# Feed-forward input products of a two-layer hybrid block: the high part of one weight unit is made ahead of the rounding of the inner values

## What is computed

```
def swiglu(h, w_in, w_out):
    g, u = jnp.split(h @ w_in, 2, axis=-1)
    return (jax.nn.silu(g) * u) @ w_out

fl = swiglu(rms_norm(xl, g_ffn_pre[i]) * (1.0 + sc2) + sh2, w_ffn_in[i], w_ffn_out[i])
xl = xl + gt2 * rms_norm(fl, g_ffn_post[i])
if need_ctx:            # the first layer only
    fc = swiglu(rms_norm(xc, g_ffn_pre[i]) * (1.0 + csc2) + csh2, w_ffn_in[i], w_ffn_out[i])
    xc = xc + cgt2 * rms_norm(fc, g_ffn_post[i])
```

## Time and profile before

| | |
|---|---|
| median of 3 runs | 1747.09 us (1743.40, 1747.09, 1752.45) |
| the profiled execution | 1751.41 us, its span 1749.6 us |
| mean granted TensorE clock | 0.991 |
| TensorE (PE) busy | 1677.9 us, 96% of the span |
| VectorE (DVE) | 709.6 us, 41% |
| ScalarE (ACT) | 641.9 us, 37% |
| GpSimd (POOL) | 678.1 us, 39% |
| chain that ended last | PE 82%, DVE 5%, issue 4%, ACT 4%, POOL 4%, DMA 1% |

### The profile page before, as it was taken

How to read it: one execution, slowest core, us unless ns; L and a number is a source line. 1 busy time by engine, 2 the same in 40 slices (tenths; PEclk the granted TensorE clock), 3 DMA queues, 4 the chain that set the end, 5 groups by cost and what they waited for, 6 DMA issues and landing times.

```text
span 1749.6 us, 25876 instructions
## 1 busy us (share of the span) xinstructions
PE 1677.9 (96%) x10242; PEld 1397.5 (80%) x10242; DVE 709.6 (41%) x1124; ACT 641.9 (37%) x1118; POOL 678.1 (39%) x454
## 2 busy tenths in 40 slices
PE   6999999999999999999899999999999999999997
PEld 4868887777877887878899878877887888888886
DVE  5135547707589635403455420015771451011103
ACT  4242126726422122213555342236762522222221
POOL 3211222038455545433542043335433444444443
PEclk9999999999999999999999999999999999999999
DMA  9553101023465645524556636432002353333331
GB/s 356 182 169 85 38 25 49 1 81 115 146 188 192 229 145 182 167 87 118 154 160 183 193 107 116 91 98 95 2 2 61 100 165 97 105 90 97 98 98 67
DMA packets 211987, 207.17 MB, mean 118 GB/s; under 512 B 16262, under 2 KB 180636, under 8 KB 211612
## 3 DMA queue, kind: packets, MB, share of 16 engines
q1 hardware_dynamic: 199208, 165.53, 31.6%
q10 hardware_dynamic: 12660, 39.99, 7.4%
HBM read 203.37 MB, written 2.13 MB: 117 GB/s over the span
## 4 chain that ended last, share of the span: by engine, by line
PE 82%; DVE 5%; issue 4%; ACT 4%; POOL 4%; DMA 1%; SPq 0%; ACTq 0%; POOLq 0%; DVEq 0%
PE ps L1722 38%; PE ps L1749 26%; PE ps L1900 3%; POOL w_lo L526 3%; PE ps L1956 3%; PE ps L2016 3%; PE ps L1921 3%; ACT w_hi L841 2%; PE ps L1796 1%; PE ps L1835 1%; DVE xs L1291 1%; DMA w_raw<-in_w_ffn_in 1%; PE ps L1968 1%; DVE hid_f L1310 1%; DMA mod_early<-in_w_mod 1%
## 5 line engine op out<-in xcount | busy, mean ns | idle before, releaser
L526 POOL TENSOR_TENSOR w_lo<-w_raw,w_hi 128x1024 fp32r<-128x1024 f32 (+1 forms) x221 | 558.5, 2529 | 892.4 <-ACT w_hi L841 892.2
L1722 PE MATMUL ps<-h_hi,w_hi 128*128 128x512 f32 (+1 forms) x1488 | 496.9, 352 | 11.9 <-POOL w_lo L526 8.1
L1722 PE MATMUL ps<-h_hi,w_lo 128*128 128x512 f32 (+1 forms) x1488 | 492.4, 349 | 0.0
L1722 PE MATMUL ps<-h_lo,w_hi 128*128 128x512 f32 (+1 forms) x1488 | 491.2, 349 | 0.0
L841 ACT ACTIVATE w_hi<-w_raw 128x1024 fp32r<-128x1024 f32 (+1 forms) x273 | 286.6, 1051 | 346.0 <-PE ps L1749 312.0
L1722 PEld LDWEIGHTS ps<-h_hi,w_hi 128*128 128x128 f32 x1488 | 269.9, 189 | 56.9 <-issue 20.8
L1722 PEld LDWEIGHTS ps<-h_hi,w_lo 128*128 128x128 f32 x1488 | 269.5, 189 | 36.1
L1722 PEld LDWEIGHTS ps<-h_lo,w_hi 128*128 128x128 f32 x1488 | 269.5, 189 | 35.7
L526 DVE TENSOR_TENSOR w_lo<-w_raw,w_hi 128x1024 fp32r<-128x1024 f32 x52 | 69.3, 1335 | 201.7 <-ACT w_hi L841 198.8
L1749 PE MATMUL ps<-w_hi,hid_hi 128*128 128x512 f32 x440 | 137.0, 393 | 8.0 <-ACT mod_row L853 4.2
L1310 DVE TENSOR_TENSOR hid_f<-silu_g,ps 128x512 f32<-128x512 f32 (+1 forms) x66 | 39.3, 595 | 254.2 <-PE ps L1722 253.8
(11 more groups left out here) (223 smaller groups left out, 1898.8 us busy)
## 6 DMA issues: line engine op xcount, KB each, us to landing
w_raw<-in_w_ffn_in SPq DMA_DIRECT2D x132, 512.0 KB, 3.8
w_raw<-in_w_ffn_out SPq DMA_DIRECT2D x66, 512.0 KB, 3.5
mod_raw<-in_w_mod ACTq DMA_DIRECT2D x42, 512.0 KB, 4.5
w_raw<-in_na_w_in SPq DMA_DIRECT2D x32, 512.0 KB, 3.7
mod_early<-in_w_mod SPq DMA_DIRECT2D x30, 512.0 KB, 9.8
full<-in_w_mod ACTq DMA_DIRECT2D x15, 512.0 KB, 5.1
w_raw<-in_ab_w_in SPq DMA_DIRECT2D x18, 256.0 KB, 5.9
w_raw<-in_ab_w_in SPq DMA_DIRECT2D x9, 512.0 KB, 8.9
```

Of the source, the lines that this page charges most:

```text
L526: eng.tensor_tensor(w_lo[:, u % RING, 0:width], w_raw[:, u % RAW, 0:width], w_hi[:, u % RING, 0:width].bitcast(F32), ALU.subtract).then_in ...
L1722: mm = pe.matmul(o[0], sta(x, o), mov(y, o), start=first and n == 0, stop=last and n == 2)
```

## The change

In ScalarE's `ffn_in` the call that makes the high part of unit s+2j+4 moves from behind the rounding `hid_hi` to in front of the wait for `hid_f`. The instructions stay the same in kind and number. The call carries its own waits: for the landing of its unit, and until TensorE has used unit s+2j+1, the up unit of the step. No transfer is issued by the moved lines. The change holds for all five input stages, 66 steps.

```
@@ -907,11 +907,10 @@
                         act.wait_ge(ff_full, f - 1)
                     act.activation(silu_g[:, f % 2, 0:width], ps(2 * (f % 2), 0, width), ACT.Silu)\
                         .then_inc(ff_silu, 1)
-                    feed(s + 2 * j + RING)
+                    feed(s + 2 * j + RING + 1)
                     act.wait_ge(ff_full, f + 1)
                     act.activation(hid_hi[:, j * width:(j + 1) * width], hid_f[:, f % 2, 0:width], ACT.Copy)\
                         .then_inc(ff_hi, 1)
-                    feed(s + 2 * j + RING + 1)
                     if hooks and j in hooks:
                         hooks[j]()
                     for m in late_loads.get((name, j), ()):
```

## The result

| | before | after |
|---|---|---|
| median of 7 runs beside each other | 1750.91 us (1743.40 to 1752.45) | 1755.59 us (1753.59 to 1758.15) |
| ratio, 95% interval | | 1.0043 (1.0026 to 1.0060) |
| profiled execution: time, span | 1751.41, 1749.6 us | 1754.93, 1753.1 us |
| mean granted clock | 0.991 | 0.989 |

The change costs 0.4% by the ratio. The two medians differ by less, 4.7 us or 0.27%, since the seven runs of before fall into two groups (1743.4 to 1747.1 and 1750.9 to 1752.5) and four of them lie in the upper one; the means differ by 7.1 us, 0.41%. In the later comparisons before's median was 1746.2 to 1747.1. The forecast was 1755.0 us, 0.45% over the median of three that it started from. Behind L908 the lines of after are one lower (L1721 is before's L1722, L1312 is L1313, L1748 is L1749).

A forecast was written before the change was run, and what follows sets the result against it. TensorE, busy 96% of the span, was taken as the bound, so changes matter only where it waits. Terms 3.4+2.5+2.2+1.1-3.9+2.6 = +7.9 us on the 1747.1 median gave 1755.0; its own range was 1750 to 1762.

The forecast's parts named there:

- Cycles of steps 0 to 7: fi0C: GpSimd's low part takes the port ahead of VectorE's urgent one, lengthening the two-step cycles; +3.4 us.
- First cycle: Steps 0 to 7 of fi0C: the odd unit TensorE waits for starts 1.9 us later, including +0.36 for hid_lo.
- Later cycles: Steps 0 to 7 of fi0C: each takes 14.9 us instead of 14.12, +0.8 in each of three.
- The doubtful step: Cycle's end in fi0C: who gets the port; requests 1.2 us apart in the steady cycle, 0.4 in the first.
- first rival: Copy is freed, port does not matter: fi0C cycle of transfer plus chain, 12.2 us; total -10.7, 1736.4 us; chance 0.13.
- Step 9: fi0C: TensorE's transposes wait longer for the modulation column that VectorE adds behind the held hid_lo; +2.5 us.
- Steps 10, 13, 16, 19: fi0C: late modulation delays silu, high part and VectorE's low part, 0.56 us short each time; +2.2 us for four.
- End of the stage: Last step of fi0C: VectorE, late from step 19, has h_lo and two low parts before the last hid_f; +1.1 us.
- Gains: fi0L: shorter mod_row waits (-0.7 twice), clock kept behind one (-1.6), shorter waits for sums (-0.9); together -3.9 us.
- Clock in `fi0C`: Longer TensorE waits in fi0C bring stretches of lower granted clock; between 0 and 5.2 us, middle taken, +2.6.
- Nothing moves: Rival: new blocks fall in slack, or fi0C losses equal the gains; 1747 us within 3; chance 0.20.
- Worse: Rival: every landing takes 5.1 us and clock is lost at all five waits; +14 to +16, 1762 us; chance 0.05.

The follow-up runs named there:

- e5_steps_0to7: New order only in steps 0 to 7 of fi0C, old order elsewhere, against the kernel before; 1747.86 us, run once.
- e1_long_only: New order only in the 512-token stages (fi0L, fi1L), old order in fi0C, against the kernel before; 1747.08 us, ratio 1.0003.
- e2_short_only: New order only in fi0C (256 tokens), old order in the other stages, against the kernel before; 1758.04 us, ratio 1.0061.
- e8_dve_first: New order in long stages and fi0C steps 0 to 7; in steps 1, 3, 5, 7 GpSimd's low part waits for VectorE's; 1737.68 us, ratio 0.9950 to before.
- e3_step9: New order only in step 9 of fi0C, old order elsewhere, against the kernel before; 1752.58 us, run once.
- e4_steps_10up: New order only in steps 10 to 21 of fi0C, old order elsewhere, against the kernel before; 1749.24 us, run once.

## Why the prediction was right

**The mechanism was the one forecast.** `hid_lo` of 128x256 is held, GpSimd's low part goes ahead of VectorE's in the first three cycles, all five waits of GpSimd's kind in `fi0C` vanish, and the column wait is 4.0. The first cycle in after, VectorE and then GpSimd:

```profile
814.22 2.44 DVE L1312 TENSOR_TENSOR hid_lo<-hid_f,hid_hi 128x256 fp32r<-128x256 f32 x1 [1.04 <-ACT hid_hi L912]
...
819.84 3.40 DVE L526 TENSOR_TENSOR w_lo<-w_raw,w_hi 128x1024 fp32r<-128x1024 f32 x1
```
```profile
819.72 2.44 POOL L526 TENSOR_TENSOR w_lo<-w_raw,w_hi 128x1024 fp32r<-128x1024 f32 x1 [2.38 <-ACT w_hi L841]
```

**Cycles of steps 0 to 7, forecast +3.4 without the clock.** e5_steps_0to7 has +3.45 from start to turn, with the turn's wait 0.15 shorter. But its waits up to the turn grew only by 1.5 us (9.3, against 7.8 in before and in e1_long_only), so some 2 us of this are slow stretches (820 to 828 at 0.80 and 0.77, 864 to 872 at 0.85 and 0.72): without them the term was too large. In after these waits even fell, from 7.8 to 6.7, and +0.7 in place with the clock in it is all that came.

First cycle: forecast +1.9, measured +1.5 (the start behind the wait lies 16.58 behind the stage's start, 15.04 in before). The term that failed is the 0.36 for `hid_lo` between the low part and the root. In after `post_norm` starts 1.01 behind the low part's end (817.38 behind 816.37), in before 0.94: `hid_lo` and the root run side by side, and it costs 0.07. Later cycles: forecast 14.9 each. The second of after takes 14.35 (838.64 to 852.99). The 0.36 is missing there too, and the moved high part starts 3.80 behind S and not 3.95, released by its landing, as forecast:

```profile
842.44 1.06 ACT L841 ACTIVATE w_hi<-w_raw 128x1024 fp32r<-128x1024 f32 x1 [0.91 <-DMA w_raw<-in_w_ffn_in]
```

In the first of these cycles, which has a stretch at 0.60 in it (824 to 828), it starts 4.70 behind S, released by TensorE's late end with the up unit, and the cycle takes 15.26:

```profile
828.08 1.06 ACT L841 ACTIVATE w_hi<-w_raw 128x1024 fp32r<-128x1024 f32 x1 [1.80 <-PE ps L1721]
```

The forecast kept the cycles and the clock apart, and they aren't: a slow stretch also delays the next chain. The doubtful step, who gets the port, fell as forecast three times in after, and the other way at the fourth:

```profile
864.33 1.22 DVE L526 TENSOR_TENSOR w_lo<-w_raw,w_hi 128x1024 fp32r<-128x1024 f32 x1
```
```profile
864.57 3.25 POOL L526 TENSOR_TENSOR w_lo<-w_raw,w_hi 128x1024 fp32r<-128x1024 f32 x1 [2.74 <-ACT w_hi L841]
```

VectorE was 0.24 us ahead, so no wait arose, and of +2.9 us at the third cycle +0.7 was left at the turn. Each engine's request follows a high part that TensorE's end released. The two ends lay 6.11 us apart here (857.32 to 863.43, with the clock at 0.76 over 856 to 860), and 5.75 in the cycle from 828.08 to 833.83. With 5.75 GpSimd would have been 0.12 ahead, as it was in that cycle. This is worked out from one trace; no run tests it. In e2_short_only GpSimd went first in all four cycles. e8_dve_first shows what this order is worth: the first rival's "transfer plus chain, 12.2 us" was forecast, and it is 12.0 when VectorE goes first. That rival was wrong in two things: `hid_lo` is held, and VectorE doesn't go first by itself.

**Step 9, forecast +2.5**: +2.33 in after, +2.2 in e3_step9.

**Steps 10, 13, 16, 19, forecast +2.2**: four waits of 0.33 or 0.34, each a start 0.49 late. In e4_steps_10up, against e1_long_only, the stretch from the turn on is 2.30 longer, 0.53 of it the wait for `hid_f`: +1.8 for the four. VectorE's low part came 2.0 later, and the slack was 1.5. **End of the stage, forecast +1.1**: 0.82 to 2.09; yet e1, e3 and e5, with the old order there, have 1.4 to 1.6, so that 0.5 to 0.7 of it is the edit's.

**Gains, forecast -3.9.** Waits for `mod_row`: -0.77 and -0.69, as forecast. The start of `fi0C` moves by -1.95 in all, so the sums and the rest gave some 0.5. The 1.6 of the clock did not come: this is the step "at 1.8 us of wait I take the clock as kept". It had been drawn from one wait of 2.5 with a slow stretch behind it, and that is a matter of chance, as e2, e3 and e5 show.

**Clock in `fi0C`, forecast +2.6, bounds 0 and 5.2**: 3.1 in after, 6.9 in e2_short_only against e1_long_only. The upper bound was too low: I had counted a slow stretch at two of five waits in full, and in e2_short_only four of the five have one.

**What made the sum fit.** Waits in `fi0C` were forecast at +9.2 with the cycles, and grew by 3.6; the clock came out near the middle; the gains were half as large; and 1.3 us fell away behind the stage, where after happened to keep the clock (1312 to 1320: 1.00, in before 0.59 over 1312 to 1316). So the profiled executions differ by 3.5 us, not 7.9: 1759.3 was forecast for this one, and it took 1754.93. The ratio of the timed runs, 1.0043, is 7.5 us on the 1747.1 that the forecast started from, since before's profiled execution was at its upper end (1751.4 in runs of 1743.4 to 1752.5) and after's at its lower one. That the direction and the port came out right is the mechanism. That the sum landed within 1 us of the median is largely luck: terms were off by 1 to 5 us in both directions. The range's upper end doesn't follow from its terms either: 1755.0 with all clock (+2.6) and slow landings (+3.3) is 1760.9, not 1762.

**Rivals.** *Nothing moves* is excluded: the interval begins at 1.0026. *Worse* decided by slow landings did not come, though e2_short_only, with 1758.0 us, reaches most of the way, by waits (+5.5) and slow stretches (6.9 us in its slowest execution).

## What to carry to other kernels

Before an operation is moved ahead on a copying engine, ask what its follower then takes: here a high part 0.7 us earlier sent a 2.4 us GpSimd instruction into the port ahead of VectorE's short ones, and the moved copy was a loss of 0.4%. With one wait that puts the urgent low part first in steps 0 to 7, and the old order from step 8 on, it became a gain of 0.4 to 0.5%. Where two engines share a port, the order of their requests has to be set by a semaphore at the places that set the end, since a lead of 0.1 or 0.2 us decides over 2.2 us here. An idle stretch of TensorE is to be counted at more than its length, with a chance, and one that can't be closed can be filled, if the filling is no longer than the wait (1.8 us gained in the one trace that shows it).

## What the runs showed of the hardware that I had not expected

- A wait of 1.84 us was followed by a product slowed by 1.6 us in all six traces, one of 2.5 us in two of five. Filled with matmuls of 1.9 us, the product was 1.8 us shorter than behind the empty wait, and even 0.2 us shorter than the 60.1 us of the same product elsewhere (59.87 and 59.91). Why the longer wait should be the milder one stays open.
- GpSimd, when its instruction started 0.12 us ahead of VectorE's next instruction (819.72 and 819.84), got the port, although VectorE's instruction stood directly behind another one of VectorE. When it started 0.24 us later, it was held for 0.85 us (3.25 for 2.40). A lead of 0.01 us was not enough: at 911.87 it was held behind `h_lo`, which started at 911.88.
- Cutting GpSimd's instruction in two lets VectorE in between, at a small price: two halves of 128x512 took 2.55 us unheld (808.25) in place of 2.40, and the ratio to before was 0.9988.
